# Second feed-forward product as seven block products per pair of token tiles instead of eight

## The chip, the cores and the metric

The kernel runs on one core of one Trainium2 chip. The time is the device time of one execution in microseconds; lower is better. All data are float32, and every large product is made from two-part operands (a rounded `hi` part and the rest, `lo`).

## The reference, cut to what matters

One decoder layer on 1024 prompt tokens and 64 sample tokens, model width 1024, feed-forward width 2816. The change touches the last product here:

```python
def swiglu(h, w1, w3, w2):
    return (jax.nn.silu(h @ w1) * (h @ w3)) @ w2

x = x + m                                   # m: the two recurrent mixers
x = x + swiglu(rmsnorm(x, norm_ffn), w1, w3, w2)
return rmsnorm(x, norm_final)
```

## The kernel before

Five engine programs are written out by hand and joined by semaphores. The first 590 us are the mixers. After them comes the feed-forward, which runs over 11 groups of 256 hidden columns (`GROUPS`); groups 1 to 9 are one hardware loop on each engine.

TensorE, one group: `hidden` does six steps. A step is one 128-column block of the hidden width (two of them) for one chunk of tokens (384, 384 or 320 columns, `FF_CHUNKS`, the last with the 64 sample tokens): 24 matmuls against w1 (`w1_step`) and 24 against w3 (`w3_step`), because each of the 8 blocks of depth takes three matmuls (`three`: hi by hi, hi by lo, lo by hi, L1753 to L1755). Then `outputs` multiplies by w2: for each of nine token tiles (`OUT_TILES`, tile 8 is the sample) and each half `q` of the 1024 output columns, two depth blocks accumulate in one PSUM bank, so 6 matmuls of 512 columns for a prompt tile and 4 for the sample. Banks 0 to 3 belong to the hidden steps, banks 4 to 7 to the outputs, in turn.

ScalarE (ACT): `silu` for each step out of PSUM, and the hi part of each weight unit (`split_w2` after step 1, `split_next` after step 5). VectorE (DVE): `gate_step` after each silu (the product with the w3 half, then the hi and lo parts of the result), `lo_of` for the lo part of a weight unit (128x2048), and `add_outputs`: one addition of 128x512 out of PSUM into the residual `x_res` (L1706) for each of the 18 output banks. TensorE may reuse an output bank when `y_dve` says that its addition is done:

```python
for q in range(2):
    m = 2 * n + q
    pe.wait_ge(y_dve, i * 18 + (m + 1))
    o = ps[:, 4 + m % 4, :]
```

SyncE loads the next weight units (1 MB each) into `raw0` and `raw1` when `lo_done` frees them. In the last group `add_outputs` puts the final norm of a finished tile (`final_norm`, L1697) between the additions, with the squares (L1144), logarithm (L707) and exponential (L709) on ACT, and SyncE stores each tile. GpSimd (POOL) has nothing to do in the feed-forward.

Of the kernel before, what the change touches and what calls it, by code (L numbers as in the profile page):

```python
# [160 lines left out]
def build(nc, x_prompt, x_sample, state_gla, state_hgrn, wstream_a, wstream_l, wstream_b, wstream_f,  # L161
          consts, pvec, w_a2, norm_final,
          y_prompt, y_sample, new_gla_p, new_hgrn_p, new_gla_s, new_hgrn_s):
    with ExitStack() as ctx:
# [94 lines left out]
        def work_part(first, width):  # L259
# [17 lines left out]

        ident = con[:, C_ID:C_ID + P]
# [24 lines left out]
        raw0_ld, raw1_ld = sem("raw0_loaded"), sem("raw1_loaded")  # L303
# [45 lines left out]
            sem("ffn_step_done"), sem("ffn_silu"), sem("ffn_gated"), sem("ffn_g_hi"), sem("ffn_g_lo"))  # L349
        y_pe, y_dve = sem("ffn_out_done"), sem("ffn_out_added")  # L350
# [11 lines left out]
        def _(sp):  # L362
# [241 lines left out]

        def wide(ap):
            return ap.rearrange("p (a d) -> p a d", a=2)

        def stage_parts(n):  # L610


            hole = p_main[:, 0:2, KTL + 2:KTL + 6, :].rearrange("p c a t -> p c (a t)")
            first = PLACE[4 * (n % 2)]
            scratch = {0: [wide(val[:, j, :]) for j in range(4)],
                       1: [wide(val[:, j, :]) for j in range(4)],
                       2: [wide(f_xn[:, j, :]) for j in range(3)] + [hole],
                       3: [wide(f_xn3[:, j, :]) for j in range(4)]}[n]
            main = [(first + j, P, scratch[j] if n == 1 else wide(x_res[:, first + j, :]), scratch[j])
                    for j in range(4)]  # L620
            s_scratch = {0: wide(val[0:NS, 4, :]), 3: wide(raw1[0:NS, 0:D])}.get(n)
            samp = (8, NS, wide(x_res[0:NS, 8, :]), s_scratch) if s_scratch is not None else None
            hi, lo = (h_hi, h_lo) if n < 2 else (f_hi, f_lo)
            return main, samp, hi, lo, HALF if n == 3 else 0, HALF if n == 0 else SEQ, V_GMIX if n < 2 else V_GFFN
# [1778 lines left out]
```

## Time and profile before

| | us |
|---|---|
| median of 3 runs | 1385.36 (1384.95 to 1385.5) |
| profiled execution, its own time | 1384.89 |
| its span, first to last instruction | 1383.1 |
| TensorE busy | 1360.7 (98%) |
| VectorE busy | 632.0 (46%) |
| ScalarE busy | 380.7 (28%) |
| GpSimd busy | 62.1 (4%) |

The profile is of one execution. The span is what its instructions cover; the execution's own time is 1.8 us longer. Busy shares are averages over all stages, and matmuls are pipelined, so TensorE's busy time counts overlapping instructions once. Line numbers (L1706) are those of the kernel before.

### The profile page before, as it was taken

To read this page: it belongs to the slowest core of one execution; us is meant where nothing else is said; L and a number is where in the kernel's file an instruction comes from. 1 tells how busy PE (TensorE), PEld (TensorE's weight loads), DVE (VectorE), ACT (ScalarE), POOL (GpSimd) and SP (SyncE) were. 2 spreads that over 40 slices of the span, in tenths; PEclk is the share of its full clock that TensorE was granted. 3 is DMA by queue.
4 is the path that set the end of the run, shared out by engine and by line. 5 is a ranking of instruction groups with operands and counts; after the bars stand their busy time and mean duration, and the time that the engine had idled before them with its cause. 6 is when DMAs were issued, how large, how long until landed. Compare 5 with 4: busy or idle time off the path is not lost.

```text
span 1383.1 us, 20842 instructions
## 1 busy us (share of the span) xinstructions
PE 1360.7 (98%) x8932; PEld 1243.5 (90%) x8932; DVE 632.0 (46%) x953; ACT 380.7 (28%) x539; POOL 62.1 (4%) x105
## 2 busy tenths in 40 slices
PE   7999999999999999999999999999999999999997
PEld 6997899988878779998999999999999999989896
DVE  4324685663236766555243433334242434252527
ACT  5226355623236555341010101010101010101115
POOL 0010322000003110000000000000000000000000
PEclk9999999999999999999999999999999999999999
DMA  5622101453132022220101010000101010101003
GB/s 185 169 79 89 64 32 64 137 164 110 64 121 94 31 91 75 95 105 31 62 31 61 30 54 25 36 37 32 59 30 61 30 61 30 61 30 61 30 1 129
DMA packets 28471, 95.14 MB, mean 69 GB/s; under 512 B 2272, under 2 KB 15872, under 8 KB 19584
## 3 DMA queue, kind: packets, MB, share of 16 engines
q1 hardware_dynamic: 28416, 94.33, 19.4%
q8 instruction: 43, 0.70, 0.2%
q14 instruction: 12, 0.10, 0.0%
HBM read 86.07 MB, written 8.00 MB: 68 GB/s over the span
## 4 chain that ended last, share of the span: by engine, by line
PE 94%; DVE 2%; DMA 1%; ACT 1%; issue 0%; SPq 0%; DVEq 0%; ACTq 0%
PE ps L1753 28%; PE ps L1755 28%; PE ps L1754 28%; PE ps L1760 1%; PE ps L1761 1%; PE ps L2082 1%; PE ps L2078 1%; PE ps L1965 1%; PE ps L2065 1%; PE ps L1791 1%; PE ps L2055 1%; PE ps L2043 1%; DMA raw<-in_wstream_a 0%; DMA x_res<-in_x_prompt 0%; DVE x_res L1697 0%; PE ps L2027 0%
## 5 line engine op out<-in xcount | busy, mean ns | idle before, releaser
L1753 PE MATMUL ps<-f_hi,whi 128*128 128x384 f32 (+1 forms) x1056 | 347.9, 329 | 0.7 <-DVE f_lo L1206 0.7
L1754 PE MATMUL ps<-f_lo,whi 128*128 128x384 f32 (+1 forms) x1056 | 347.7, 329 | 0.0
L1755 PE MATMUL ps<-f_hi,wlo 128*128 128x384 f32 (+1 forms) x1056 | 347.6, 329 | 0.0
L1675 DVE TENSOR_TENSOR gated<-gated,ps 128x384 f32<-128x384 f32 (+1 forms) x66 | 35.1, 532 | 400.1 <-ACT gated L1092 400.1
L1092 ACT ACTIVATE gated<-ps 128x384 f32<-128x384 f32 (+1 forms) x66 | 31.3, 475 | 664.5 <-PE ps L1755 664.5
L1753 PEld LDWEIGHTS ps<-f_hi,whi 128*128 128x128 f32 x1056 | 198.4, 188 | 1.5 <-DVE f_lo L1206 1.0
L1754 PEld LDWEIGHTS ps<-f_lo,whi 128*128 128x128 f32 x1056 | 198.4, 188 | 0.5
L1755 PEld LDWEIGHTS ps<-f_hi,wlo 128*128 128x128 f32 x1056 | 198.4, 188 | 0.0
L1706 DVE TENSOR_TENSOR x_res<-ps,x_res 128x512 f32<-128x512 f32 x198 | 132.6, 688 | 63.8 <-PE ps L1755 63.8
L1753 PE MATMUL ps<-h_hi,whi 128*128 128x320 f32 (+2 forms) x464 | 155.6, 335 | 0.4 <-DVE h_lo L1206 0.4
L1755 PE MATMUL ps<-h_hi,wlo 128*128 128x320 f32 (+2 forms) x464 | 153.3, 330 | 0.0
L1754 PE MATMUL ps<-h_lo,whi 128*128 128x320 f32 (+2 forms) x464 | 153.2, 330 | 0.0
L1754 PE MATMUL ps<-wlo,g_hi 128*128 128x512 f32 x352 | 137.2, 390 | 0.0
L1753 PE MATMUL ps<-whi,g_hi 128*128 128x512 f32 x352 | 137.1, 390 | 0.0
L1755 PE MATMUL ps<-whi,g_lo 128*128 128x512 f32 x352 | 137.0, 389 | 0.0
L1753 PEld LDWEIGHTS ps<-h_hi,whi 128*128 128x128 f32 x464 | 87.4, 188 | 8.2 <-DVE h_lo L1206 0.7
L1755 PEld LDWEIGHTS ps<-h_hi,wlo 128*128 128x128 f32 x464 | 87.4, 188 | 7.3
L1754 PEld LDWEIGHTS ps<-h_lo,whi 128*128 128x128 f32 x464 | 87.5, 189 | 6.9
L1755 PEld LDWEIGHTS ps<-whi,g_lo 128*128 128x128 f32 x352 | 66.1, 188 | 13.9
L1753 PEld LDWEIGHTS ps<-whi,g_hi 128*128 128x128 f32 x352 | 66.1, 188 | 13.5
L1754 PEld LDWEIGHTS ps<-wlo,g_hi 128*128 128x128 f32 x352 | 66.1, 188 | 13.3
L1172 DVE TENSOR_TENSOR wlo<-raw,whi 128x2048 fp32r<-128x2048 f32 (+1 forms) x28 | 60.9, 2174 | 36.0 <-ACT whi L702 36.0
(277 smaller groups left out, 1841.2 us busy)
## 6 DMA issues: line engine op xcount, KB each, us to landing
raw<-in_wstream_f SPq DMA_DIRECT2D x33, 1024.0 KB, 4.8
raw<-in_wstream_a SPq DMA_DIRECT2D x19, 1024.0 KB, 4.8
raw<-in_wstream_b SPq DMA_DIRECT2D x16, 1024.0 KB, 4.8
x_res<-in_x_prompt SPq DMA_DIRECT2D x12, 512.0 KB, 5.0
out_y_prompt<-x_res SPq DMA_DIRECT2D x7, 512.0 KB, 2.6
x_res<-in_state_hgrn SPq DMA_DIRECT2D x4, 512.0 KB, 8.7
val<-in_x_prompt SPq DMA_DIRECT2D x4, 512.0 KB, 8.2
out_new_hgrn_s<-x_res SPq DMA_DIRECT2D x4, 512.0 KB, 5.1
```

The lines of the kernel that those rows point to most:

```text
L1092: nc.scalar.activation(gated[:, st % 2, 0:w], ps[:, 2 * (st % 2), 0:w], ACT.Silu).then_inc(silu_f, 1)
L1172: nc.vector.tensor_tensor(wlo[s][:, first:size], raw_of(u)[:, first:size], whi[s][:, first:size].bitcast(F32), ALU.subtract).then_inc(lo_d ...
L1675: nc.vector.tensor_tensor(gated[:, s, 0:w], gated[:, s, 0:w], ps[:, 2 * s + 1, 0:w], ALU.mult).then_inc(gm_done, 1)
L1706: nc.vector.tensor_tensor(x, ps[:, 4 + m % 4, :], x, ALU.add).then_inc(y_dve, 1)
L1753: nc.tensor.matmul(out, a_hi, b_hi, start=first, stop=False)
L1754: nc.tensor.matmul(out, a_hi, b_lo, start=False, stop=False)
L1755: return nc.tensor.matmul(out, a_lo, b_hi, start=False, stop=last)
L1760: nc.tensor.matmul(out, a, b_hi, start=first, stop=False)
L1761: return nc.tensor.matmul(out, a, b_lo, start=False, stop=last)
L1791: last = nc.tensor.transpose(ps[:, bank, j * P:(j + 1) * P], scratch[:, k // 4, (k % 4) * P:(k % 4 + 1) * P], ident)
L1965: nc.tensor.matmul(ps[:, g, :].rearrange("p (n t) -> p n t", n=4), ones, sum_place(C, g), start=True, stop=True).then_inc(ss_pe, 1)
L2043: nc.tensor.matmul(ps[a:a + 32, g, o + a:o + a + 32], p_main[r, c, KTL + slot, a:a + 32], p_main[r, c, QT + slot, a:a + 32], start=True, s ...
```

## The change

Strassen's algorithm over blocks of two by two by two. The two token tiles of a pair, the two depth blocks of the group and the two halves of the output columns give seven products of 128x128 by 128x512 (three matmuls each) where there were eight. The pairs are tiles (0, 3), (1, 4), (2, 5) and (6, 7). The blocks of the activations (`g_all`: 4 blocks and the sums S1 to S4) and of w2 (3 blocks and the sums T1 to T4 in `w2_all`) are added on DVE; hi parts are made on ACT, lo parts on DVE. Each product is added to the residual where it belongs, ten additions for a pair instead of eight (table `ADDED`: product, tile of the pair, half, earlier addition that it waits for). Each product fills a bank of its own (banks 4 to 7 in turn), products 4 to 6 of a pair wait for the additions of products 0 to 2 of the same pair, and products 0 to 3 of the next for those of 3 to 6. Two of the four quarters of a pair are held in changed form (POOL subtracts once ahead of the feed-forward and changes them back at the end, DVE for the last pair). The sample tile uses the seven weight blocks too: 8 matmuls as before. The order of TensorE in a group is: steps 0 and 1, pair 3 and sample of the group before, steps 2 to 4, pair 0, step 5, pairs 1 and 2. In the last group the pairs' order is 3 and sample (of the group before), 0, 1, step 5, pair 2, sample, pair 3. `raw1` is gone: w1, w3 and w2 units take turns in `raw0`.

```diff
+PAIRS = [(0, 3), (1, 4), (2, 5), (6, 7)]
+PRODUCTS = [(A11, B11), (S1, T1), (S3, T3), (A12, B21), (S2, T2), (A22, T4), (S4, B22)]
+ADDED = [(0, 0, 0, 0), (0, 1, 1, 0), (1, 1, 0, 0), (1, 1, 1, 2), (2, 0, 1, 0), (2, 1, 1, 4), (3, 0, 0, 1),
+         (4, 1, 1, 6), (5, 1, 0, 3), (6, 0, 1, 5)]
+PAIR_PE, PAIR_DVE = 7, 10
...
+            def split_w1(i):
+                act.wait_ge(raw0_ld, i * 48 + 16 * (F0_UNIT + 3))
+                act.wait_ge(w1_used, i + 1)
                 nc.scalar.activation(whi[0][:], raw0[:], ACT.Copy).then_inc(hi_done, 1)
...
+            def ffn_group(i, first=False, last=False):
+                for st in range(5):
+                    if st or not first:
+                        silu(i, st)
+                    if st < 4:
+                        blocks_hi(i, st)
                     if st == 1:
                         split_w2(i)
+                if not last:
+                    split_w1(i)
+                    silu(i, 5)
+                    split_w3(i)
+                    blocks_hi(i, 5)
...
+            def add_pair(i, p, pe_at, dve_at):
+                tiles = [x_res[:, PLACE[t], :] for t in PAIRS[p]]
+                for j, e, q, dep in ADDED:
+                    dve.wait_ge(y_pe, i * Y_PE + (pe_at + j + 1))
+                    if dep:
+                        dve.wait_ge(y_dve, i * Y_DVE + (dve_at + dep))
+                    x = tiles[e][:, 512 * q:512 * (q + 1)]
+                    nc.vector.tensor_tensor(x, ps[:, bank_of(pe_at, j), :], x, ALU.add).then_inc(y_dve, 1)
...
+            def second_part(i):
+                w2_sums(i)
+                gate_step(i, 2)
+                w2_lows(i)
+                gate_step(i, 3)
+                gate_step(i, 4)
+                add_pair(i, 0, 0, 0)
+
+            def next_weights(i):
+                lo_of(0, raw0, i * 3 + (F0_UNIT + 4))
+                for p in (1, 2):
+                    add_pair(i, p, p * PAIR_PE, p * PAIR_DVE)
+                lo_of(1, raw0, i * 3 + (F0_UNIT + 5))
+                gate_step(i, 5)
...
             with dve.Fori(1, GROUPS - 1) as i:
-                ffn_group(i, False)
+                gate_step(i, 0)
+                gate_step(i, 1)
+                add_rest(i)
+                second_part(i)
+                next_weights(i)
+            end = GROUPS - 1
+            gate_step(end, 0)
+            gate_step(end, 1)
+            add_rest(end)
+            second_part(end)
+            add_pair(end, 1, PAIR_PE, PAIR_DVE)
+            gate_step(end, 5)
             dve.wait_ge(nf_ld, 16)
-            ffn_group(GROUPS - 1, True)
+            final_norm(0)
+            add_pair(end, 2, 2 * PAIR_PE, 2 * PAIR_DVE)
+            final_norm(1)
+            add_sample(end, 3 * PAIR_PE, (0, 1))
+            final_norm(2)
+            add_pair(end, 3, 3 * PAIR_PE + 2, 3 * PAIR_DVE + 2)
...
+            def pair(i, p, pe_at, dve_at, ahead=None, first=False):
...
+                for j, (s, t) in enumerate(PRODUCTS):
...
+                    if j >= 4:
+                        pe.wait_ge(y_dve, i * Y_DVE + (dve_at + (2, 4, 6)[j - 4]))
+                    elif ahead is not None:
+                        pe.wait_ge(y_dve, i * Y_DVE + (ahead + (7, 8, 9, 10)[j]))
...
+                    three(ps[:, bank_of(pe_at, j), :], g_hi[:, s, a], g_lo[:, s, a], w2_hi[:, t, :], w2_lo[:, t, :],
+                          True, True).then_inc(y_pe, 1)
```

How the change moves instructions, at three places.

TensorE, `outputs` before, inside the loop over the groups: the sample's second half and the first product of the tile after it (`whi` holds the hi part of w2 here, `ffn_out_added` is `y_dve`).

```order
L2285 REGISTER_ALU
L1760 MATMUL ps<-whi,g_samp 128x512 [waits ffn_out_added]
L1761 MATMUL ps<-wlo,g_samp 128x512
L1760 MATMUL ps<-whi,g_samp 128x512
L1761 MATMUL ps<-wlo,g_samp 128x512
L2285 REGISTER_ALU
L1753 MATMUL ps<-whi,g_hi 128x512 [waits ffn_out_added]
```

TensorE, pair 0 in the loop of the change, from the end of its product 3 to step 5 (L1920 to L1922 are the three matmuls of `three`).

```order
L1921 MATMUL ps<-w_lo,g_hi 128x512
L1922 MATMUL ps<-w_hi,g_lo 128x512
L2454 REGISTER_ALU
L1920 MATMUL ps<-w_hi,g_hi 128x512 [waits ffn_out_added]
L1921 MATMUL ps<-w_lo,g_hi 128x512
L1922 MATMUL ps<-w_hi,g_lo 128x512
L2454 REGISTER_ALU
L1920 MATMUL ps<-w_hi,g_hi 128x512 [waits ffn_out_added]
L1921 MATMUL ps<-w_lo,g_hi 128x512
L1922 MATMUL ps<-w_hi,g_lo 128x512
```

A bank now carries three matmuls instead of six (or four) between two waits on DVE's additions.

DVE, the same loop of the change, the first rows of `second_part`'s end and of pair 0 (L1830 is the addition, L1779 and L1781 the gate of step 4, `con` holds the sample's hidden values).

```order
L1779 TENSOR_TENSOR g_all<-g_all,ps 128x2x128 [waits ffn_silu]
L1781 TENSOR_TENSOR con<-con,ps 128x64
L1783 REGISTER_ALU
L1752 TENSOR_TENSOR g_all<-g_all 128x128 [waits ffn_gated]
L1826 REGISTER_ALU
L1830 TENSOR_TENSOR x_res<-ps,x_res 128x512 [waits ffn_out_done] x2
L1826 REGISTER_ALU
L1830 TENSOR_TENSOR x_res<-ps,x_res 128x512 [waits ffn_out_done]
L1828 REGISTER_ALU [waits ffn_out_done]
L1830 TENSOR_TENSOR x_res<-ps,x_res 128x512 [waits ffn_out_added]
```

The gate of step 4, three instructions, stands ahead of the ten additions of pair 0. Before, the additions stood behind the gate of step 5 and had one wait each.

DVE, last group of the change, from the end of the gate of step 5 to the first sample additions (L1845 is `final_norm`).

```order
L1756 TENSOR_TENSOR g_lo<-g_all,g_hi 128x7x128 [waits ffn_g_hi]
L1800 TENSOR_TENSOR g_samp<-con,g_samp 128x2x64 [waits ffn_sample_hi]
L1801 TENSOR_TENSOR g_sum<-con,g_sum 128x64
L1845 SCALAR_TENSOR_TENSOR x_res<-x_res,small,raw 128x1024 [waits final_rstd,norm_final_loaded]
L1830 TENSOR_TENSOR x_res<-ps,x_res 128x512 [waits ffn_out_done] x3
L1830 TENSOR_TENSOR x_res<-ps,x_res 128x512 [waits ffn_out_added,ffn_out_done]
L1830 TENSOR_TENSOR x_res<-ps,x_res 128x512 [waits ffn_out_done]
L1830 TENSOR_TENSOR x_res<-ps,x_res 128x512 [waits ffn_out_added,ffn_out_done] x5
L1845 SCALAR_TENSOR_TENSOR x_res<-x_res,small,raw 128x1024 [waits final_rstd]
L1836 TENSOR_TENSOR x_res<-ps,x_res 128x512 [waits ffn_out_done] x2
```

The first final norm, which waits for ACT's statistics, now stands ahead of pair 2's additions; before, each norm stood behind the two additions of a later tile.

## Rows read from the trace of the kernel before

**Rows 1.** The page: busy us, share of the span and instructions of each engine.

```profile
PE 1360.7 (98%) x8932; PEld 1243.5 (90%) x8932; DVE 632.0 (46%) x953; ACT 380.7 (28%) x539; POOL 62.1 (4%) x105
```

**Rows 2.** Waits, 600 to 1384 us: who waited for whom, us, times, longest.

```profile
DVE x_res L1706 <- PE ps L1755: 63.8, 107, 0.7
...
PE ps L1753 <- DVE f_lo L1206: 0.7, 1, 0.7
```

**Rows 3.** Stretches of one loop group: length, busy PE, PEld, DVE, ACT, POOL, clock, DMA.

```profile
739.48:811.11 71.63, 71.63 (x394) 67.53 (x393) 27.27 (x44) 8.26 (x9) 0.00 (x0) 1.00 0.12 44
```

**Rows 4.** Timeline around 800 us: start us, us, engine, operation [idle before <-releaser].

```profile
799.85 0.39 PE L1753 MATMUL ps<-whi,g_hi 128*128 128x512 f32 x1
...
800.31 0.39 PE L1755 MATMUL ps<-whi,g_lo 128*128 128x512 f32 x1
...
800.73 0.69 DVE L1706 TENSOR_TENSOR x_res<-ps,x_res 128x512 f32<-128x512 f32 x1 [0.61 <-PE ps L1755]
...
801.21 0.39 PE L1753 MATMUL ps<-whi,g_hi 128*128 128x512 f32 x1
```

**Rows 5.** Timeline of DVE, same group: additions in a row, weight lo, gate.

```profile
739.48 0.56 DVE L1675 TENSOR_TENSOR gated<-gated,ps 128x384 f32<-128x384 f32 x1 [8.31 <-ACT gated L1092]
...
772.86 0.43 DVE L1687 TENSOR_TENSOR g_lo<-gated,g_hi 128x256 fp32r<-128x256 f32 x1
773.20 0.22 DVE L1687 TENSOR_TENSOR g_samp<-gated,g_samp 128x64 fp32r<-128x64 f32 x1
...
795.45 2.28 DVE L1663 TENSOR_TENSOR wlo<-raw,whi 128x2048 fp32r<-128x2048 f32 x1
797.65 2.48 DVE L1706 TENSOR_TENSOR x_res<-ps,x_res 128x512 f32<-128x512 f32 x4
```

**Rows 6.** Timeline of ACT, same group: silus of steps 0, 1, 4, 5; weight hi.

```profile
738.96 0.49 ACT L1092 ACTIVATE gated<-ps 128x384 f32<-128x384 f32 x1 [28.06 <-PE ps L1755]
747.44 0.49 ACT L1092 ACTIVATE gated<-ps 128x384 f32<-128x384 f32 x1 [7.99 <-PE ps L1755]
747.82 1.91 ACT L1097 ACTIVATE whi<-raw 128x2048 fp32r<-128x2048 f32 x1
...
771.44 0.44 ACT L1092 ACTIVATE gated<-ps 128x320 f32<-128x320 f32 x1 [6.55 <-PE ps L1755]
778.48 0.44 ACT L1092 ACTIVATE gated<-ps 128x320 f32<-128x320 f32 x1 [6.61 <-PE ps L1755]
```

**Rows 7.** Timeline at 526 us: TensorE resumes after waiting for DVE.

```profile
525.79 1.23 DVE L1238 TENSOR_TENSOR pr_main<-p_main,pr_main 128x1024 fp32r<-128x1024 f32 x1 [0.25 <-ACT pr_main L801]
...
527.07 0.38 PE L1753 MATMUL ps<-whi,pr_main 128*128 128x256 f32 x1
...
527.29 0.28 PE L1754 MATMUL ps<-wlo,pr_main 128*128 128x256 f32 x1
...
527.41 0.28 PE L1755 MATMUL ps<-whi,pr_main 128*128 128x256 f32 x1
```

**Rows 8.** Timeline of the last group's end.

```profile
1351.95 1.28 ACT L1129 ACT_TABLE_LOAD   x1
...
1373.36 1.06 ACT L1144 ACTIVATE raw<-x_res 128x1024 f32<-128x1024 f32 x1 [1.33 <-DVE x_res L1706]
...
1374.68 0.39 PE L1755 MATMUL ps<-whi,g_lo 128*128 128x512 f32 x1
...
1375.11 1.28 DVE L1697 SCALAR_TENSOR_TENSOR x_res<-x_res,small,nf 128x1024 f32<-128x1024 f32 x1
...
1378.85 1.41 DVE L1697 SCALAR_TENSOR_TENSOR x_res<-x_res,small,nf 128x512 f32<-128x512 f32 x2 [0.60 <-ACT small L709]
```

**Rows 9.** Stretches behind TensorE's last matmul, columns as in rows 3.

```profile
1376.00:1378.00 2.00, 0.00 (x0) 0.00 (x0) 2.00 (x3) 1.84 (x8) 0.00 (x0) 0.98 0.38 158
1378.00:1380.00 2.00, 0.00 (x0) 0.00 (x0) 1.40 (x4) 0.50 (x2) 0.00 (x0) 0.50 0.58 176
```

**Rows 10.** POOL's groups by shape: names, shapes, count, busy us, mean ns of one, idle before.

```profile
L602 POOL TENSOR_TENSOR kT_st<-p_samp 128x512 f32<-128x512 f32 x1 | 1.3, 1271 | 50.8 <-DVE p_samp L1620 50.8
```

More of the change, by code:

```diff
@@ L173, in build @@
         pv = tensor(ctx, "pv", [P, V_ALL])
+        with ExitStack() as later:
+            g_sum = tensor(later, "g_sum", [P, 2, NS], F32R)
         wa2 = tensor(ctx, "wa2", [RANK2, HA * KA])
@@ L302, in build @@
         xr_ld = sem("x_reloaded")
[L303 removed]
+        raw0_ld = sem("raw0_loaded")
         st_ld = sem("sample_states_loaded")
@@ L603, in _, with change_back @@
                                             p_samp[:, GT:GT + NH, :], ALU.mult).then_inc(s_og, 1)
[L607 to L624, printed above, removed]
-        N_STAGES = 4
-        def turn_bank(n, k):
-            return [1, (6, 4)[k % 2], (2, 3)[k % 2], 4 + k % 4][n]
-        def tiles_before(n):
-            return sum(len(stage_parts(m)[0]) + bool(stage_parts(m)[1]) for m in range(n))
+            pairs = [[x_res[:, PLACE[t], :] for t in pair] for pair in PAIRS]
+            pool.wait_ge(xn_done, tiles_before(N_STAGES))
+            for x1, x2 in pairs:
+                nc.gpsimd.tensor_tensor(x2[:, 0:512], x2[:, 512:D], x2[:, 0:512], ALU.subtract).then_inc(xt_done, 1)
+                nc.gpsimd.tensor_tensor(x1[:, 512:D], x2[:, 512:D], x1[:, 512:D], ALU.subtract).then_inc(xt_done, 1)
+            def change_back(p):
+                x1, x2 = pairs[p]
+                end = GROUPS - 1
+                for m, x in enumerate((x2[:, 0:512], x1[:, 512:D])):
+                    pool.wait_ge(y_dve, end * Y_DVE + p * PAIR_DVE + 9 + m)
+                    nc.gpsimd.tensor_tensor(x, x2[:, 512:D], x, ALU.subtract).then_inc(post_pool, 1)
+            for p in range(3):
+                change_back(p)
         def turns_before(n):
@@ new lines, in blocks_hi @@
+            def blocks_hi(i, st):
+                if st < 2:
+                    act.wait_ge(gm_done, i * 6 + (st + 3))
+                else:
+                    act.wait_ge(gc_done, i * 8 + {2: 1, 3: 4, 5: 8}[st])
+                first, end, cols = {0: (A11, A12, MAIN), 1: (A12, S3, MAIN), 2: (S3, A22, MAIN),
+                                    3: (A22, 7, MAIN), 5: (0, 7, REST)}[st]
+                nc.scalar.activation(g_hi[:, first:end, cols], g_all[:, first:end, cols], ACT.Copy).then_inc(gh_done, 1)
@@ L1143, in _ @@
                 if n < 8:
-                    nc.scalar.activation(raw1[0:rows, 0:D], x_res[0:rows, PLACE[t], :], ACT.Square,
+                    nc.scalar.activation(y_junk[0:rows], x_res[0:rows, PLACE[t], :], ACT.Square,
                                          accum_out=ms[0:rows, t:t + 1]).then_inc(sqf, 1)
@@ new lines, in sample_outputs, with product @@
+            def sample_outputs(i, banks, ahead):
+                x = [v.rearrange("p e t -> p (e t)") for v in (g_samp[:, 0], g_samp[:, 1], g_sum[:])]
+                def product(q, k, t, start):
+                    return both(ps[:, banks[q], :], x[k], w2_hi[:, t, :], w2_lo[:, t, :], start, not start)
+                if ahead is not None:
+                    pe.wait_ge(y_dve, i * Y_DVE + (ahead + 7))
+                product(0, 0, B11, True)
+                product(0, 1, B21, False).then_inc(y_pe, 1)
+                if ahead is not None:
+                    pe.wait_ge(y_dve, i * Y_DVE + (ahead + 8))
+                product(1, 2, B22, True)
+                product(1, 0, T3, False).then_inc(y_pe, 1)
```

349 lines of the change are left out of this document (223 added, 126 removed).

## Prediction

> **What bounds the kernel now.** I read the page first: TensorE is busy for 98% of the span, no other engine for half of it [rows 1]. Then the list of waits of the feed-forward half: TensorE waits for DVE once, 0.7 us, at its beginning, and DVE waits for TensorE 107 times, never over 0.7 us [rows 2]. Then one loop group: 71.63 us long, TensorE busy all of it at a granted clock of 1.00 (the level of 2.4 GHz), DVE busy for 27.27 us and ACT for 8.26 us [rows 3]. So TensorE alone bounds this stage, and what counts is how long its list of matmuls is and whether anybody begins to hold it up.
>
> Six matmuls of 512 columns, two products of three, start over 1.36 us [rows 4], so one is 0.2267 us and a product of the change 0.68 us. A step with 384 columns is 747.44 - 738.96 = 8.48 us, one with 320 is 778.48 - 771.44 = 7.04 us [rows 6]. An addition out of PSUM takes 0.69 us alone, and four in a row take 2.48 us, so they start 0.60 us apart [rows 5]. It begins 0.42 us after the start of the last matmul that it waits for [rows 4], which is 0.87 us after the start of a product of three.
>
> **What TensorE sheds.** A pair of tiles takes 21 matmuls instead of 24, the sample 8 as before: 12 fewer in a group, 12 x 0.2267 = 2.72 us, and in 11 groups **29.9 us less**. Those are all on the path.
>
> **What DVE gets.** 42 additions in a group where there were 18, 24 more x 0.60 = 14.4 us, and the sums for T, S and their lo parts. Its 27 us become some 47 of 71: it stays far from full on average, so the average says nothing. What matters is the burst. Products 0, 1 and 2 of a pair have two additions each, and the bank of each is wanted again by products 4, 5 and 6. TensorE makes a product in 0.68 us, DVE clears such a bank in 1.20.
>
> Let P be the start of a pair on TensorE and P + d that of its first addition. The sixth addition starts at d + 5 x 0.60 and ends 0.69 later. TensorE resumes 0.05 us behind DVE's end (525.79 + 1.23 = 527.02, and 527.07), and the weight load that could not be made ahead costs 0.10 more (the next matmul follows after 0.22 instead of 0.12) [rows 7]. So product 6 starts at d + 3.85 instead of 6 x 0.68 = 4.08, and **a pair loses d - 0.23 us**. The four pairs of a loop group differ in d alone:
> - Pair 1. DVE comes from the lo part of w1, whose hi part waits for the middle of step 5. Half a step is 3.52 us, 0.2 to ACT, 1.91 us [rows 6], a hand-over of 0.04, then 2.2 us of DVE [rows 5]: 7.9 us after the start of step 5. The first addition wants to begin at 7.04 + 0.87 = 7.9: hidden, just. d = 0.87, loss 0.64.
> - Pair 2 follows pair 1 at once. DVE needs ten additions, 6.02 us, from 0.87 on, thus to 6.89; TensorE is at 4.76 + 0.64 = 5.40. d = 1.49, loss 1.26.
> - Pair 3, of the group before, stands behind step 1, and on DVE behind the gate of step 1: silu from 0.20 us, 0.49 long [rows 6], a hand-over of 0.04, the gate 0.47 to the next start. d = 1.20, loss 0.97.
> - Pair 0 stands behind step 4, whose gate is three instructions behind two silus: 0.20, ACT 0.50 (between the rows for 320 columns and for nothing), then gates of 256 and 64 and a subtraction of 128 columns, 0.33 + 0.22 + 0.20 with two hand-overs, by the rows for 256 and 64 [rows 5]. d = 1.54, loss 1.31.
>
> Sum **4.18 us lost in a group against 2.72 saved: 1.46 us longer**, a loop group of 73.1 us. Nine of them: +13.1 us. The first group has pairs 0 to 2 only: 3.2 lost; its wait for the changed residuals lies on POOL, eight subtractions at 1.27 us [rows 10], 10 us, beside steps 0 and 1, which take 17; I take nothing and allow 0 to 3.
>
> **The last group.** Pair 3 of the group before loses 0.97, pair 0 1.31, pair 1 directly behind it 1.26. Then comes step 5 and pair 2, and here DVE has a longer list ahead of the additions. From P of pair 2: the gate of step 5 and its sums by 2.5, hi parts on ACT to 3.4, the table load of 1.28 (DVE meanwhile does the lo parts), then from the start of the square to that of the norm 1375.11 - 1373.36 = 1.75, and 1.2 for the norm itself [rows 8]. d = 7.4: TensorE stands for **7.2 us** behind four full banks. The sample takes 1.8 us. Before pair 3 DVE has ten additions, a norm, two additions and a norm, 9.6 us from 7.4, that is 17.0; TensorE is there at 4.76 + 7.2 + 1.8 = 13.8. d = 3.2, loss 3.0. Sum 13.7 us.
>
> **Behind the last matmul.** Before, the last matmul starts at 1374.68, so its slot ends at 1374.91; DVE's last norm ends at 1380.26: 5.35 us [rows 8]. Now, from the end of the last product: DVE adds until 1.5 us later, then changes two quarters back (1.2), three norms of 1.2, the fold of the sample (1.2), and from there three times ACT's statistics before a norm (about 1.8, 1.6 and, with the two half squares and their sum, 2.2, and 1.2 between), some 14 us in all. **+8.7 us.** The store behind it is the same.
>
> **The sum.** -29.9 (matmuls) + 3.2 + 9 x 4.18 + 13.7 (waits, 54.5) + 8.7 (end) = **+33.3 us**. The profiled execution took 1384.9 us, so it gives 1418.2; the median of the runs shown is 0.5 above that execution. I forecast **1418.7 us**, 2.4% slower.
>
> **Covers that are thin.** With one buffer for the weights, w3's lo part comes behind pair 2's additions: it is done at d + 6.02 + 2.28, 3.8 us after pair 2's end on TensorE, and is wanted at the middle of step 0, 4.24. The lo parts of S for pair 0 are done about 6.4 us after step 3 and wanted at 7.04. Both hold, by 0.4 and 0.6 us. The loads (1 MB) have 15 us and more each. If one is missed by 1 us in each group, 10 us come on top.
>
> **A page against the rows.** The rows show additions 0.60 us apart though each lasts 0.69 [rows 5]. The sum above rests on that. The Trainium skill, VectorE: DVE Perf Modes, section The DRAIN you can't avoid, says that the next DVE instruction does not start until the pipe of the one before is empty. By that rule additions would stand 0.69 apart; it is one of the rivals below, and [rows 5] speak against it.
>
> In the gap of 7 us in the last group TensorE is idle. After its last matmul the granted clock was 0.98 from 1376 to 1378 and 0.50, the level of 1.2 GHz, from 1378 on [rows 9], with the engine idle since 1375. So it may fall in the gap too. The products behind it wait for additions anyway; only if it stayed low to the end would the ten products' 7.5 us double, and half of that lies behind DVE's list. 0 to 4 us, taken as 0.5, within the rounding.
>
> **Rivals.**
> 1. DVE's additions do not overlap. Four of ten wait for an earlier addition of their own engine, besides TensorE, which no addition in these rows does. At 0.69 apart an isolated pair loses 0.45 us more and pair 2 more again, 2.5 us a group and 28 in all: 1447. With a hand-over on each, 0.73, 1461. If only the four marked ones do so, 1434. For it: the new waits. Against it: the wait is for an addition two or more places back, which is over by then.
> 2. A thin cover breaks, weights or lo parts: +10, 1429.
> 3. The other side: TensorE never waits for the banks. It decides at one point: additions 0.48 us apart or less, or d near 0.23. Then only the matmuls go (-29.9), with the last group's gap and end left (7.2 + 3.0 + 8.7): 1374, **faster** by 11 us. At 0.55 apart a loop group would be even. Against it: 0.60 stands in every row of consecutive additions.
> 4. The change does not shed its matmuls: the instruction lists show three matmuls between bank waits, so no.
>
> **Numbers.** The forecast's own case 0.68, 1410 to 1428 (d off by 0.2 us in each of 43 pairs is 9 us). Rival 1 0.20, rival 2 0.08, rival 3 0.04. The range takes in the forecast's case, rival 2 and most of rival 1: 1405 to 1445. A measurement of this kernel tells about 0.2% from no change. Slower by more than that 0.95, within it 0.01, faster 0.04.
>
> **What the profile after would show.** Right: loop groups of 73 us; waits of TensorE for DVE's additions before products 4 to 6, three or so in each pair, none over 0.7 us but in the last group; additions 0.60 us apart inside a pair; in the last group one gap of some 7 us; 17 us from the last matmul's slot to the end. Wrong: loop groups near 69 us with no such waits (rival 3); additions 0.69 us apart and groups of 75 us or more (rival 1); waits of TensorE at the beginning of a step for a weight's lo part (rival 2).

## The result and the profile after

| | us |
|---|---|
| before, median of 4 runs | 1385.28 (1384.95 to 1385.5) |
| the change, median of 4 runs | 1414.03 (1413.72 to 1415.45) |
| ratio | 1.021, 95% interval 1.0192 to 1.0227 |
| profiled execution of the change, its own time | 1414.03 |
| its span | 1412.2 |

The change is slower by 28.75 us. Against the profiled execution of before the span grew by 1412.2 - 1383.1 = 29.1 us.

The page of the change, busy us, share of the span and instructions of each engine, and two rows of its costliest groups:

```profile
PE 1358.0 (96%) x8800; PEld 1207.7 (86%) x8800; DVE 860.2 (61%) x1307; ACT 445.4 (32%) x638; POOL 80.7 (6%) x119
...
L1830 DVE TENSOR_TENSOR x_res<-ps,x_res 128x512 f32<-128x512 f32 x440 | 266.1, 681 | 0.1
...
L1920 PEld LDWEIGHTS ps<-w_hi,g_hi 128*128 128x128 f32 x308 | 58.0, 188 | 74.9 <-DVE x_res L1830 67.4
```

Beside [rows 1], TensorE has 8800 matmuls instead of 8932: the 132 x 0.2267 = 29.9 us are gone from its list. Its busy time fell by only 2.7 us, because the records cover part of each wait: a matmul is shown for 0.39 us though the next one may start after 0.2267, so the first 0.16 us of a wait lie under the record ahead of it, and the matmul behind a late weight load is shown longer (0.50 us). The 440 additions, now at L1830, hardly ever leave a hole in front of themselves (0.1 us in all), and the weight loads of the products stood 67.4 us behind them.

The waits of the feed-forward half of the change, 600 to 1420 us (who waited for whom: us, times, longest):

```profile
PEld ps L1920 <- DVE x_res L1830: 67.4, 112, 6.5
...
PE ps L1920 <- DVE x_res L1830: 21.9, 69, 6.1
...
PE ps L1920 <- DVE f_lo L1289: 0.7, 1, 0.7
```

In [rows 2] TensorE waited only once. Now its row for the additions says 21.9 us, and even that is too little, for the reason just given: of the wait before product 6 of the pair below, 0.23 us are shown as idle, while by the starts it costs 0.50. The starts of the matmuls tell the price of a wait, so the losses below are read from them.

Stretches of the first four loop groups (columns as in [rows 3]):

```profile
661.43:733.85 72.42, 70.91 (x382) 63.86 (x381) 47.78 (x76) 14.21 (x18) 0.00 (x0) 1.00 0.13 44
733.85:806.42 72.57, 71.05 (x382) 64.01 (x381) 47.78 (x76) 14.20 (x18) 0.00 (x0) 1.00 0.12 43
806.42:879.16 72.74, 71.24 (x382) 64.17 (x381) 47.79 (x76) 14.21 (x18) 0.00 (x0) 1.00 0.12 43
879.16:952.07 72.91, 71.39 (x382) 64.32 (x381) 47.80 (x76) 14.21 (x18) 0.00 (x0) 1.00 0.13 43
```

A loop group took 71.63 us [rows 3], with 394 matmul records where there are 382 now. DVE works 47.8 us of it instead of 27.3, at the same clock.

TensorE's timeline of one pair in the first of these groups (pair 3; only the first matmuls of products 0, 4, 5 and 6, then the sample's first):

```profile
669.03 0.39 PE L1920 MATMUL ps<-w_hi,g_hi 128*128 128x512 f32 x1
...
671.77 0.39 PE L1920 MATMUL ps<-w_hi,g_hi 128*128 128x512 f32 x1
...
672.76 0.50 PE L1920 MATMUL ps<-w_hi,g_hi 128*128 128x512 f32 x1
...
673.95 0.50 PE L1920 MATMUL ps<-w_hi,g_hi 128*128 128x512 f32 x1 [0.23 <-DVE x_res L1830]
...
674.76 0.39 PE L1927 MATMUL ps<-w_hi,g_samp 128*128 128x512 f32 x1
```

and DVE's: pair 3, pair 0, then pair 1 with the first eight additions of pair 2 (the view ends there):

```profile
670.23 6.07 DVE L1830 TENSOR_TENSOR x_res<-ps,x_res 128x512 f32<-128x512 f32 x10
...
701.81 6.07 DVE L1830 TENSOR_TENSOR x_res<-ps,x_res 128x512 f32<-128x512 f32 x10
...
714.29 10.86 DVE L1830 TENSOR_TENSOR x_res<-ps,x_res 128x512 f32<-128x512 f32 x18
```

Products 5 and 6 start 1.19 us apart, which is the time of two additions, not of three matmuls (0.68). The pair takes 674.76 - 669.03 = 5.73 us where its matmuls need 4.76: 0.97 lost. Ten additions take 6.07 us, thus start (6.07 - 0.69) / 9 = 0.598 us apart.

TensorE in the last group: pair 2's products 0 and 3, products 4 and 5 behind the gap, the sample, pair 3's first and last matmul.

```profile
1373.02 0.40 PE L1920 MATMUL ps<-w_hi,g_hi 128*128 128x512 f32 x1
...
1375.56 0.39 PE L1922 MATMUL ps<-w_hi,g_lo 128*128 128x512 f32 x1
1382.07 0.79 PE L1920 MATMUL ps<-w_hi,g_hi 128*128 128x512 f32 x1 [6.12 <-DVE x_res L1830]
1382.66 0.63 PE L1921 MATMUL ps<-w_lo,g_hi 128*128 128x512 f32 x1
...
1386.07 0.63 PE L1927 MATMUL ps<-w_hi,g_samp 128*128 128x512 f32 x1
...
1388.90 0.39 PE L1920 MATMUL ps<-w_hi,g_hi 128*128 128x512 f32 x1
...
1395.25 0.39 PE L1922 MATMUL ps<-w_hi,g_lo 128*128 128x512 f32 x1
```

DVE in the same stretch and to the end:

```profile
1379.53 1.28 DVE L1845 SCALAR_TENSOR_TENSOR x_res<-x_res,small,raw 128x1024 f32<-128x1024 f32 x1 [1.66 <-ACT small L767]
1380.73 6.28 DVE L1830 TENSOR_TENSOR x_res<-ps,x_res 128x512 f32<-128x512 f32 x10
...
1390.95 6.06 DVE L1830 TENSOR_TENSOR x_res<-ps,x_res 128x512 f32<-128x512 f32 x10
...
1408.29 1.41 DVE L1845 SCALAR_TENSOR_TENSOR x_res<-x_res,small,raw 128x512 f32<-128x512 f32 x2 [0.60 <-ACT small L767]
```

And three stretches there (the clock stands third from the end, as in [rows 9]):

```profile
1376.00:1378.00 2.00, 0.00 (x0) 0.00 (x0) 1.43 (x3) 1.97 (x3) 0.00 (x0) 0.99 0.00 0
1378.00:1380.00 2.00, 0.00 (x0) 0.00 (x0) 0.47 (x1) 1.94 (x5) 0.00 (x0) 0.50 0.00 0
1384.00:1386.00 2.00, 2.00 (x6) 1.54 (x5) 2.00 (x4) 0.20 (x1) 0.00 (x0) 0.50 0.00 0
```

Pair 2's first addition waits for a norm, the norm for ACT; TensorE stands from 1375.8 to 1382.07 and comes back at half the clock, 0.43 us from matmul to matmul, until 1388.2. From the last product's slot (1395.25 + 0.23) to DVE's end (1408.29 + 1.41) are 14.2 us, where [rows 8] had 5.35.

### The profile page after: what moved, and what is told of

Its sections match the earlier page's. It is cut to its first block, busy times and chain, and to the rows that moved or that the text cites. A ratio compares the mean times of both kernels' runs of the same rounds, so it can differ in the third digit from the quotient of the medians.

```text
span 1412.2 us, 21629 instructions
## 1 busy us (share of the span) xinstructions
PE 1358.0 (96%) x8800; PEld 1207.7 (86%) x8800; DVE 860.2 (61%) x1307; ACT 445.4 (32%) x638; POOL 80.7 (6%) x119
## 4 chain that ended last, share of the span: by engine, by line
PE 83%; DVE 9%; issue 3%; ACT 2%; DMA 1%; DVEq 0%; SPq 0%; ACTq 0%
PE ps L1920 25%; PE ps L1922 24%; PE ps L1921 24%; DVE x_res L1830 6%; PE ps L1927 1%; PE ps L1928 1%; PE ps L2249 1%; PE ps L2245 1%; PE ps L2132 1%; PE ps L2232 1%; DVE x_res L1845 1%; PE ps L2222 1%; PE ps L1958 1%; PE ps L2210 1%; DMA raw<-in_wstream_a 0%
## 5 line engine op out<-in xcount | busy, mean ns | idle before, releaser
L1920 PE MATMUL ps<-f_hi,whi 128*128 128x384 f32 (+1 forms) x1056 | 346.3, 328 | 0.7 <-DVE f_lo L1289 0.7
L1922 PE MATMUL ps<-f_hi,wlo 128*128 128x384 f32 (+1 forms) x1056 | 345.9, 328 | 0.0
L1830 DVE TENSOR_TENSOR x_res<-ps,x_res 128x512 f32<-128x512 f32 x440 | 266.1, 681 | 0.1
L1920 PEld LDWEIGHTS ps<-f_hi,whi 128*128 128x128 f32 x1056 | 198.5, 188 | 2.5 <-DVE f_lo L1289 1.0
L1922 PEld LDWEIGHTS ps<-f_hi,wlo 128*128 128x128 f32 x1056 | 198.5, 188 | 0.0
L1920 PE MATMUL ps<-h_hi,whi 128*128 128x320 f32 (+2 forms) x464 | 155.6, 335 | 0.4 <-DVE h_lo L1289 0.4
L1920 PE MATMUL ps<-w_hi,g_hi 128*128 128x512 f32 x308 | 133.0, 432 | 23.1 <-DVE x_res L1830 21.9
L1922 PE MATMUL ps<-h_hi,wlo 128*128 128x320 f32 (+2 forms) x464 | 153.4, 331 | 0.0
L1776 DVE TENSOR_TENSOR g_all<-g_all,ps 128x384 f32<-128x384 f32 x44 | 24.4, 555 | 192.0 <-ACT g_all L1150 192.0
L1920 PEld LDWEIGHTS ps<-w_hi,g_hi 128*128 128x128 f32 x308 | 58.0, 188 | 74.9 <-DVE x_res L1830 67.4
L1921 PE MATMUL ps<-w_lo,g_hi 128*128 128x512 f32 x308 | 121.8, 395 | 0.0
L1922 PE MATMUL ps<-w_hi,g_lo 128*128 128x512 f32 x308 | 121.6, 395 | 0.0
L1920 PEld LDWEIGHTS ps<-h_hi,whi 128*128 128x128 f32 x464 | 87.4, 188 | 8.2 <-DVE h_lo L1289 0.7
L1922 PEld LDWEIGHTS ps<-h_hi,wlo 128*128 128x128 f32 x464 | 87.4, 188 | 7.3
L1162 ACT ACTIVATE g_hi<-g_all 128x384 fp32r<-128x384 f32 (+2 forms) x55 | 44.3, 805 | 144.3 <-DVE g_all L1752 131.3
L1150 ACT ACTIVATE g_all<-ps 128x384 f32<-128x384 f32 x44 | 21.6, 491 | 179.1 <-PE ps L1922 179.1
L1920 PE MATMUL ps<-whi,pr_main 128*128 128x256 f32 x256 | 74.7, 292 | 1.3 <-DVE pr_main L1321 1.0
```

What stands on the lines that cost most here:

```text
L1150: nc.scalar.activation(g_all[:, b, MAIN], ps[:, 2 * s, MAIN], ACT.Silu).then_inc(silu_f, 1)
L1162: nc.scalar.activation(g_hi[:, first:end, cols], g_all[:, first:end, cols], ACT.Copy).then_inc(gh_done, 1)
L1776: nc.vector.tensor_tensor(x, x, ps[:, 2 * s + 1, MAIN], ALU.mult).then_inc(gm_done, 1)
L1830: nc.vector.tensor_tensor(x, ps[:, bank_of(pe_at, j), :], x, ALU.add).then_inc(y_dve, 1)
L1920: nc.tensor.matmul(out, a_hi, b_hi, start=first, stop=False)
L1921: nc.tensor.matmul(out, a_hi, b_lo, start=False, stop=False)
```

## The experiments

Ten kernels. Each ratio is against the kernel before, run on the same chip in the same series (its medians there: 1384.45, 1384.93 and 1384.23 us).

### 1. Only seven additions

The second additions of products 0, 1 and 2 are left out, so this kernel does not compute the whole product. The matmuls, sums and waits stay.

```diff
-ADDED = [(0, 0, 0, 0), (0, 1, 1, 0), (1, 1, 0, 0), (1, 1, 1, 2), (2, 0, 1, 0), (2, 1, 1, 4), (3, 0, 0, 1),
-         (4, 1, 1, 6), (5, 1, 0, 3), (6, 0, 1, 5)]
-PAIR_PE, PAIR_DVE = 7, 10
+ADDED = [(0, 0, 0, 0), (1, 1, 0, 0), (2, 0, 1, 0), (3, 0, 0, 1), (4, 1, 1, 0), (5, 1, 0, 2), (6, 0, 1, 3)]
+PAIR_PE, PAIR_DVE = 7, 7
+CLEARED = (1, 2, 3, 4, 5, 6, 7)
```

> The second additions of products 0, 1 and 2 are left out (7 additions for a pair instead of 10), so that every output bank is cleared by one addition; matmuls, sums, loads and order stay. Theory (TensorE waits because two additions of 0.60 us clear a bank that it wants back after 0.68): the waits before products 4 to 6 vanish, a loop group is 68.9 us (0.2 to 0.6 less where the 384-column matmuls start 173 ns apart instead of 177), the whole about 1366 us, 48 less than the change. Rival A (the added sums, hi and lo parts or the single weight buffer hold TensorE up): groups stay at 72 us or more and the time within 10 us of 1414. Rival B (DVE's own additions wait for each other): the time falls only to about 1395.

Measured: 1371.49 us, ratio 0.9906 (0.9889 to 0.9922), faster than before. The expectation had 1366 us. TensorE's waits from 640 to 1345 us, and the first loop group:

```profile
PE ps L1920 <- DVE x_res L1830: 5.5, 1, 5.5
```

```profile
657.26:725.97 68.71, 68.71 (x382) 64.95 (x381) 42.09 (x63) 14.20 (x18) 0.00 (x0) 1.00 0.14 46
```

No loop group has a wait (the one of 5.5 us stands in the last group), and a group is 68.71 us against 72.42 to 72.91. So in the loop the sums, gates and loads that the change added do not hold TensorE up by themselves; without the second additions every wait is gone. The whole kernel is 42.5 us faster than the change; nine loop groups of 4.0 account for 36 of them. The groups came as expected (68.9), so the 5.5 us that are missing lie outside the loop.

### 2. The same ten additions, spread

The question was whether the number of additions costs the time or where they stand. The products are made in another order (old 3, 4, 0, 5, 1, 2, 6), so that those with two additions are not the first three.

```diff
-PRODUCTS = [(A11, B11), (S1, T1), (S3, T3), (A12, B21), (S2, T2), (A22, T4), (S4, B22)]
+PRODUCTS = [(A12, B21), (S2, T2), (A11, B11), (A22, T4), (S1, T1), (S3, T3), (S4, B22)]
...
+CLEARED = (1, 2, 4, 5, 7, 9, 10)
...
-                        pe.wait_ge(y_dve, i * Y_DVE + (dve_at + (2, 4, 6)[j - 4]))
+                        pe.wait_ge(y_dve, i * Y_DVE + (dve_at + CLEARED[j - 4]))
```

> The same seven products and ten additions, but in the order 3, 4, 0, 5, 1, 2, 6: one addition for the first two products, so that products 4, 5 and 6 wait for the first, second and fourth addition instead of the second, fourth and sixth. DVE's work is the same to the instruction. Theory (the burst at the head of a pair): pairs 0, 1 and 3 lose nearly nothing, pair 2 behind pair 1 keeps some 0.3 us, a loop group is 70.6 us (up to 0.6 less by the matmul spacing), the whole about 1389 us. Rival (DVE's total of additions is what counts): same as the change, 1414.

Measured: 1393.88 us, ratio 1.0067 (1.005 to 1.0084): 20 us of the change's 29 are back with no work removed, less than expected (1389). A new wait stands in the trace (640 to 1345 us):

```profile
PE ps L1920 <- DVE wlo L1746: 6.2, 10, 0.7
PE ps L1920 <- DVE x_res L1830: 2.5, 11, 0.2
```

TensorE hardly stands in the pairs any more, comes to step 0 earlier, and finds the lo part of w3 not ready, ten times. This is the prediction's second rival; in the change the loss in the pairs had kept it away. Read from the starts, pairs 3 and 0 of a loop group now lose 0.01 and 0.10 us instead of 0.97 and 1.30, but pairs 1 and 2 together still 0.97 (1.90 before the edit) where the theory had 0.3. A loop group takes 70.59 us. That is the expected 70.6, which was more than the theory's own terms give (68.9 and 0.3, so 69.2): the wait of 0.6 and the loss in pairs 1 and 2 fill most of the difference. So the 5 us by which the whole missed 1389 lie outside the loop and are not assigned.

### 3. The last group's order on DVE

Pair 2's additions come before the first norm, and the sample's fold before the norms that need nothing of it.

```diff
             gate_step(end, 5)
             dve.wait_ge(nf_ld, 16)
-            final_norm(0)
             add_pair(end, 2, 2 * PAIR_PE, 2 * PAIR_DVE)
-            final_norm(1)
+            final_norm(0)
             add_sample(end, 3 * PAIR_PE, (0, 1))
-            final_norm(2)
+            final_norm(1)
             add_pair(end, 3, 3 * PAIR_PE + 2, 3 * PAIR_DVE + 2)
...
-            for n in (3, 4, 5):
-                final_norm(n)
             fold(2, y_fold)
+            for n in (2, 3, 4, 5):
+                final_norm(n)
```

> Only the end of the last group is reordered on DVE: pair 2's additions come ahead of the first final norm, and the sample's fold ahead of the last six norms instead of between them; loop groups as in the change. Theory (the 6 us gap of TensorE and the long end cost what the trace of the change shows): TensorE's gap in the last group shrinks from 6.1 to about 4 us, the end from the last matmul's slot to the last store by some 1 to 2 us, the whole 1410 us, 4 less than the change. Rival (the end is bound by DVE's list from the gate of step 5 on, whatever its order): 1413 to 1414.

Measured: 1411.09 us (1408.0 to 1411.58), ratio 1.0183 (1.0165 to 1.02), 2.9 us below the change. TensorE's longest wait fell from 6.1 to 3.2 us. Pair 2's first addition comes 4.76 us after the pair's first matmul (1378.20 - 1373.44) instead of 7.71: the edit took 3.0 us out of this d, and the time fell by as much. What is left of d is step 5's gate with its sums and its hi and lo parts, which stand ahead of the additions in either order.

### 4. Both together

The edits of experiments 2 and 3 in one kernel.

> Both edits, the spread order of products and the reordered end. Theory: the gains add, 25 and 4 us, about 1385 us, the time of the kernel before. Rival: they overlap or one hides the other, 1388 or more.

Measured: 1391.77 us, ratio 1.0048 (1.0031 to 1.0065), against 1385 expected. The expectation had added up 25 us for the new order and 4 for the end, where experiments 2 and 3 give 20 and 3 alone; together they give 22.3. The wait for w3's lo part is here too (6.1 us).

### 5. Spread further, and w3's lo part in halves

On top of experiment 4: the products' order is now old 3, 4, 5, 0, 1, 6, 2. The lo part of w3 is made in two halves, and the first half of step 0's w3 matmuls waits for the first alone.

```diff
-PRODUCTS = [(A11, B11), (S1, T1), (S3, T3), (A12, B21), (S2, T2), (A22, T4), (S4, B22)]
...
+PRODUCTS = [(A12, B21), (S2, T2), (A22, T4), (A11, B11), (S1, T1), (S4, B22), (S3, T3)]
...
+CLEARED = (1, 2, 3, 5, 7, 8, 10)
...
-                lo_of(1, raw0, i * 3 + (F0_UNIT + 5))
+                dve.wait_ge(hi_done, i * 3 + (F0_UNIT + 5))
+                for part, done in ((slice(0, 1024), w3_half), (slice(1024, 2048), lo_done)):
+                    nc.vector.tensor_tensor(wlo[1][:, part], raw0[:, part], whi[1][:, part].bitcast(F32),
+                                            ALU.subtract).then_inc(done, 1)
...
+                        pe.wait_ge(w3_half, i)
+                        w3_step(st, 0, 4)
                         pe.wait_ge(lo_done, i * 3 + (F0_UNIT + 2))
+                        w3_step(st, 4)
```

> As spread_last, with two more edits: the order of products is 3, 4, 5, 0, 1, 6, 2, and DVE makes the lo part of w3 in two halves of 128x1024, the first of which releases TensorE for the first half of step 0's w3 matmuls. Theory (the 0.6 us in each group that TensorE waits in spread and spread_last for the lo part of w3, DVE being 5 us behind after pair 2, is a cover that broke when the additions stopped holding TensorE up): that wait goes, a loop group is 69.6 us against 70.6, the whole about 1382 us, 10 less than spread_last. Rival (DVE is full behind pair 2, and what the halves give comes back as waits for additions): within 2 us of 1392.

Measured: 1377.86 us, ratio 0.9955 (0.9938 to 0.9971), 4 us better than expected and **below the kernel before**. From 640 to 1345 us the only wait of TensorE for DVE, and the first two loop groups:

```profile
PE ps L1923 <- DVE x_res L1831: 0.2, 1, 0.2
```

```profile
658.91:728.13 69.22, 69.08 (x382) 64.43 (x381) 48.05 (x77) 14.20 (x19) 0.00 (x0) 1.00 0.13 47
728.13:797.65 69.52, 69.39 (x382) 64.67 (x381) 48.05 (x77) 14.20 (x18) 0.00 (x0) 1.00 0.13 45
```

DVE has all ten additions and is busy for 48 of 69 us, and TensorE hardly waits. It does still lose a little that this row does not show: the first matmul of pair 1 and, 42 matmuls later, the first of step 0 in the first of these groups are

```profile
709.18 0.40 PE L1923 MATMUL ps<-w_hi,g_hi 128*128 128x512 f32 x1
...
719.43 0.34 PE L1923 MATMUL ps<-f_hi,whi 128*128 128x384 f32 x1
```

which is 10.25 us where the matmuls need 9.52, so 0.73 lost; pairs 3 and 0 lose 0.01 and 0.05. Four pairs lose 0.8 us in a group instead of 4.2, with the same ten additions each. The burst was the cost, not the load. The two edits were made together and no run has one without the other; the rows tell them apart only in so far as the wait for w3's lo part is gone and pairs 1 and 2 lose 0.73 instead of experiment 2's 0.97.

### 6. Norms while TensorE still works

On top of experiment 5: ACT's statistics and DVE's norms of pair 0's two tiles come while step 5 runs, ahead of its gate. The edit on ACT, which puts those statistics and a table load ahead of step 5's silu, is left out here.

```diff
             add_pair(end, 1, PAIR_PE, PAIR_DVE)
-            gate_step(end, 5)
             dve.wait_ge(nf_ld, 16)
-            add_pair(end, 2, 2 * PAIR_PE, 2 * PAIR_DVE)
             final_norm(0)
+            final_norm(1)
+            gate_step(end, 5)
+            add_pair(end, 2, 2 * PAIR_PE, 2 * PAIR_DVE)
             add_sample(end, 3 * PAIR_PE, (0, 1))
-            final_norm(1)
+            final_norm(2)
```

> As half, and in the last group the statistics and final norms of pair 0's two tiles are done while TensorE computes step 5, where DVE and ACT stand idle for 6 us, instead of behind it. Theory (the end is bound by DVE's list behind the gate of step 5): two norms of 1.2 us leave that list, the whole 2.4 us less than half, about 1379 us. Rival (the end is bound by the chain of the last tiles' statistics): same as half.

Measured: 1375.88 us (1374.42 to 1376.89), ratio 0.9936 (0.9919 to 0.9952): **the fastest kernel with the whole computation**, 9 us under before, 38 under the change. DVE's timeline in the last group, from those two norms to pair 2's additions:

```profile
1337.97 3.51 DVE L1853 SCALAR_TENSOR_TENSOR x_res<-x_res,small,raw 128x1024 f32<-128x1024 f32 x2
1342.79 0.42 DVE L1787 TENSOR_TENSOR g_all<-g_all,ps 128x256 f32<-128x256 f32 x1 [1.30 <-ACT con L1154]
...
1346.82 6.06 DVE L1838 TENSOR_TENSOR x_res<-ps,x_res 128x512 f32<-128x512 f32 x10
```

The two norms fill what was a hole of 4.71 us before step 5's gate in experiment 5 (6.24 in the change) and is now 1.30. The gain over experiment 5 is 2.0 us (expected 2.4).

### 7. Step 4's gate behind pair 0's additions

```diff
-                gate_step(i, 4)
                 add_pair(i, 0, 0, 0)
+                gate_step(i, 4)
```

This tests the term d by itself: pair 0's additions no longer stand behind three gate instructions.

> The change with one edit: on DVE the gate of step 4 stands behind pair 0's ten additions instead of ahead of them. Theory (a pair loses the time from its start to its first addition less 0.23 us): pair 0's first addition starts 0.87 us behind its first matmul instead of 1.5, so a group loses 0.6 us less, the whole is 7 us less than the change, about 1407. Rival (the gate's place does not matter since step 5 gives DVE time to catch up): 1414.

Measured: 1407.14 us (1405.48 to 1410.28), ratio 1.0161 (1.0144 to 1.0178), 6.9 us below the change; expected 1407. The pair's d is 701.90 - 701.00 = 0.90 us instead of 1.53, and from step 4 to step 5 are 12.47 us instead of 13.10: both fell by 0.63, which is "loses d - 0.23" seen in one term. It is so in the first ten groups. In the last, pair 1 follows pair 0 at once and the gate now stands between their additions: the two pairs take 12.33 us there instead of 12.04.

### 8. A short stand in the kernel before

In the traces, runs of 384-column matmuls start on average either 173.3 or 176.7 ns apart (in the second kind, one start comes after about 174 and the next after about 179), and in the kernel before and the change each run is of one kind throughout: a step of 48 takes 8.32 or 8.48 us. The kernel before has the wider one in every loop group [rows 6]. Here TensorE waits, ahead of each pass of its loop, for its own products of the pass before.

```diff
+                pe.wait_ge(y_pe, i * 18)
                 hidden(i, range(6))
```

> The kernel before with one wait more: at the head of each pass of the loop over the groups TensorE waits for the end of its own last product. In the kernel before all 192 matmuls of 384 columns of a loop group start 176.7 ns apart; in the change, behind waits, 14 of 20 such runs start 173.3 ns apart, which is 4.5 us in all. Theory (a short stand of TensorE ahead of a run can bring it into the faster spacing): runs at 173.3 ns, 0.64 us less in a group, against some 0.35 us for the wait, the whole 2 to 3 us less than the kernel before, 1382 us. Rival (the spacing is set by the loop itself or by what came before it): spacing stays 176.7 ns and the wait is paid, 1388 us.

Measured: 1382.77 us over 10 runs, ratio 0.9984 (0.9975 to 0.9994). Silu of steps 0 to 2 in one group, on ACT:

```profile
738.73 0.49 ACT L1092 ACTIVATE gated<-ps 128x384 f32<-128x384 f32 x1 [28.29 <-PE ps L1755]
747.05 0.49 ACT L1092 ACTIVATE gated<-ps 128x384 f32<-128x384 f32 x1 [7.83 <-PE ps L1755]
...
755.37 0.49 ACT L1092 ACTIVATE gated<-ps 128x384 f32<-128x384 f32 x1 [6.03 <-PE ps L1755]
```

Steps are 8.32 us apart in every loop group, where [rows 6] has 8.48; the last group, outside the loop and without the wait, keeps 8.48. The wait costs 0.31 us a group (658.20 us to 658.74 from the last product's matmul to the first of the steps, where 0.23 is usual) and 0.10 more for the first weight load, and four faster steps give back 0.64: 0.23 a group. A loop group takes 71.38 us instead of 71.63, and the kernel became 2.2 us faster.

A stand is not the only thing that brings the shorter spacing: in experiment 1 no loop group has a wait, and steps 2 and 3 start 173.3 ns apart in all of them, while in experiment 6 they start 176.7 ns apart in all.

### 9. The gap filled with matmuls

Is the half clock behind the gap a cost? Between products 3 and 4 of the last group's pair 2 stand 24 matmuls of 512 columns into a free bank, whose result nobody reads.

```diff
+                    if j == 4 and fill:
+                        pe.wait_ge(gm_done, i * 6 + 7)
+                        for n in range(fill):
+                            nc.tensor.matmul(ps[:, 0, :], g_hi[:, 0, a], w2_hi[:, 0, :], start=True, stop=True)
```

> The change with 24 matmuls of 512 columns added on TensorE in the last group, between products 3 and 4 of pair 2, where it stands for 6 us; they write a bank that nobody reads before it is written anew. In the change the granted clock fell in that stand and products 4 to 6 and the sample ran at 1.2 GHz. Theory (the slow clock cost nothing, since DVE's additions and norms set the end): the clock stays at 1.00, the sample's matmuls are done some 2 us earlier, the whole stays within 1.5 us of 1414. Rival (the slow clock cost what it doubled): 2 to 4 us less than the change, 1411.

Measured: 1413.7 us (1411.94 to 1414.45), ratio 1.0209 (1.0195 to 1.0223), 0.3 us below the change, which is nothing that can be told. Its stretches:

```profile
1378.00:1380.00 2.00, 2.00 (x11) 1.65 (x10) 0.85 (x1) 1.94 (x6) 0.00 (x0) 1.00 0.00 0
...
1390.00:1392.00 2.00, 0.10 (x1) 0.10 (x1) 2.00 (x4) 1.94 (x5) 0.00 (x0) 1.00 0.44 180
...
1394.00:1396.00 2.00, 1.99 (x5) 0.88 (x3) 2.00 (x4) 0.00 (x0) 0.00 (x0) 0.50 0.00 0
```

The clock stays at 1.00 through the old gap, and pair 3's first matmul comes at 1386.75 instead of 1388.90. But 0.39 us of that were there before the gap (step 5's gate starts on DVE at 1373.36 instead of 1373.75), and DVE is busy from pair 2's additions on, so pair 3's first addition comes at 1390.58 instead of 1390.95, no sooner behind that gate. TensorE's gain goes into a longer wait before its product 4, 2.24 us instead of 0.50, after which the clock falls for the last products. From step 5's gate to DVE's last norm are 36.07 us, and 35.95 in the change. There the time belongs to DVE.

### 10. The short stand in the fastest kernel

```diff
+                pe.wait_ge(y_pe, i * Y_PE)
                 hidden(i, range(2, 5))
```

> The kernel best with one more wait in the loop: behind the sample's products, ahead of steps 2 and 3, TensorE waits for the end of its own last product. In best the 96 matmuls of steps 2 and 3 started 176.7 ns apart in all groups. Theory (a short stand ahead of a run brings the faster spacing): they start 173.3 ns apart, which gives 0.32 us a group and costs about as much for the wait: the time stays within 1 us of 1376. Rival (that wait does nothing to this run): spacing 176.7 ns and 3 us more, 1379.

Measured: 1376.87 us (1375.35 to 1378.68), ratio 0.9947 (0.9933 to 0.996), not told apart from experiment 6. In eight of nine loop groups step 3 now comes 8.32 us behind step 2 instead of 8.48, but the interval ahead of it, from step 1 to step 2, which holds the stand, grew from 15.08 to some 15.35 us. That is 0.27 us more against 0.16 less, in each group: the stand takes more than the two faster steps give back.

## Why the prediction was right

It forecast 1418.7 us, slower; measured 1414.03. Step by step:

- **A pair loses d - 0.23 us.** Right, and shown by the rows below and by experiments 1, 2, 5 and 7. In the first loop group:

| pair | d forecast | d | loss forecast | loss |
|---|---|---|---|---|
| 3 | 1.20 | 1.20 | 0.97 | 0.97 |
| 0 | 1.54 | 1.53 | 1.31 | 1.30 |
| 1 | 0.87 | 0.91 | 0.64 | 0.68 |
| 2 | 1.49 | 1.46 | 1.26 | 1.22 |
| sum | | | 4.18 | 4.17 |

- **The matmuls shed, -29.9 us.** Right in count. What failed is a term that was not there at all: the working took a step of 384 columns as 8.48 us in both kernels. In the change 14 of 20 such runs (two steps each) have the spacing of 173.3 ns, 0.32 us less each, 4.5 us in all. That is why loop groups took 72.4 to 72.9 us and not 73.1, and it accounts for nearly all of the 4.2 to 4.7 us between forecast and measurement.
- **The last group, 13.7 us.** Measured 14.6: pairs 3, 0 and 1 taken at 3.5, pair 2 8.3 (forecast 7.2: d was 7.71, not 7.4, and products 4 to 6 ran at half the clock), the sample 1.0 more than its 1.8, pair 3 1.8 (forecast 3.0, since TensorE came to it later). The sum was off by 0.9, its parts by up to 1.2 either way, so that it came so near is in part luck.
- **The end, +8.7.** Measured 14.2 - 5.35 = 8.85.
- **The clock in the gap, 0 to 4 us, taken as 0.5.** The 0.5 stands in none of the sum's terms. The clock fell to 0.50 as allowed, and stretched pair 2 and the sample on TensorE (in the 14.6 above); experiment 9 shows that keeping it up behind the gap gains nothing that can be measured.
- **The sum.** -29.9 - 4.5 + 3.2 (first group, as forecast, and without the wait for POOL that was allowed for) + 37.5 (nine times 4.17) + 14.6 + 8.85 = 29.75, against 29.1 measured. The 0.65 left is not assigned.
- **Rival 1, additions that don't overlap.** Refuted: ten take 6.07 us, by 0.69 they would take 6.9, and among them are the four that wait for earlier additions. The rule it was weighed with (the Trainium skill, VectorE: DVE Perf Modes, section The DRAIN you can't avoid) is only half of what that section says: it adds that a next instruction that is not held starts earlier. The trace shows that half, 0.598 us from start to start at 0.69 us each.
- **Rival 2, a thin cover breaks.** Not in the change, but in experiments 2 and 4 as soon as TensorE stopped waiting in the pairs: ten waits, 6.2 us. The margin of 0.4 us was worked out against a TensorE that was late.
- **Rival 3, TensorE never waits for the banks.** Wrong for the change. Experiment 1 is that case in the loop, and experiment 5 comes near it (0.8 us lost in a group): 1371.5 and 1377.9 us, where the rival had 1374.
- **What it did not see:** the cost lay in the order of the products, not in the algorithm. The prediction named the burst and yet priced only the order as it stood.
- **The signs that it named.** Groups of 72.4 to 72.9 us (73), one gap of 6.1 us (some 7), additions 0.60 us apart, 1412.2 - 1395.48 = 16.7 us from the last slot to the end (17), and in the loop no wait of TensorE over 0.7 us.

## What to carry to other kernels

When matmuls are traded for additions out of PSUM, cost the burst, not the average: count for each bank how long the clearing engine takes against how long the next product needs, and put the products with two additions apart before giving the trade up. Here the same arithmetic, in another order on TensorE and DVE and with one subtraction split in two, went from 29 us slower to 9 us faster. After each wait removed, work out again the margins that were measured against the late engine.

## What the runs showed of the hardware

- **Two spacings of the same matmuls.** At a granted clock of 1.00, matmuls of 384 columns start on average 173.3 or 176.7 ns apart; those of 320 always 146.7, those of 512 mostly 226.7. Behind a stand of about 0.3 us ahead of the run it was the shorter one in nine of nine groups in experiment 8 and in eight of nine in experiment 10, and in experiment 1 the shorter one came for steps 2 and 3 without a stand. What sets it stays open.
- **The clock in a gap.** TensorE idle from 1375.8 us: granted 0.99 until 1378, then 0.50, and 0.50 still while it worked from 1382 to 1388. The Trainium skill, TensorE: Matmul & The Clock Gate, section What's actually happening, says that activity releases the throttle and idleness brings it back, which the trace bears out. Keeping the clock up there gained nothing (experiment 9), since DVE's list set the pace.
- **A wait is worth more than its row.** The record ahead of a wait covers its first 0.16 us (0.39 shown, 0.2267 to the next start when nothing waits), and behind it a 512-column matmul is shown as 0.50 us instead of 0.39, so TensorE's own waits in the change sum to 21.9 us, while the starts give nine times 4.17, 37.5 us, in the loop alone.
